# Later slots for one head's attention products and delta chain, and its DMA transposes issued from ScalarE's queue

## The reference

```
h = rms_norm(x); one projection h @ w_in gives, for each of 8 heads of width 128,
   q, k, v, gate path of a causal attention (with 256 tokens there is one block: plain causal softmax with ALiBi)
   q, k, v, gate path of a gated delta rule (short causal conv + SiLU on q, k, v), and two merge gates of 2048
A: softmax(q k^T - slope * distance) v * silu(z)                       -> ya, 1024 wide
B: delta rule in chunks, per-head rms_norm * silu(z)                   -> yb, 1024 wide
merged = sigmoid(g_a) * (ya @ w_branch_a) + sigmoid(g_b) * (yb @ w_branch_b)
out = rms_norm(x + merged @ w_out)
```

## Time and profile before

| | |
|---|---|
| median of 3 runs | 788.77 us (787.17 to 788.86) |
| the profiled execution's own time | 788.17 us, of which its span is 786.4 us |
| TensorE's granted clock | 0.998 of full speed over the span |
| busy: PE, DVE, ACT, POOL | 764.7, 553.3, 467.6, 102.1 us |
| moved by DMA | 152.89 MB, at a mean of 194 GB/s |

### The profile page before, as it was taken

One profiled execution on the slowest core, in us unless ns is written; L12 is line 12 of the kernel. 1 busy time (PEld: TensorE's weight loads), 2 busy tenths in 40 slices (PEclk: granted clock), 3 DMA queues, 4 the chain that ended last, 5 costly groups with the idle time before them and its releaser, 6 DMA issues.

```text
span 786.4 us, 10433 instructions
## 1 busy us (share of the span) xinstructions
PE 764.7 (97%) x3507; PEld 627.6 (80%) x3507; DVE 553.3 (70%) x1265; ACT 467.6 (59%) x697; POOL 102.1 (13%) x167
## 2 busy tenths in 40 slices
PE   8998999999999999999999999999999999999996
PEld 6887887888788878878887788788778888888884
DVE  5779748965895698479658956884797566765563
ACT  5686557656764766477567556764765764435440
POOL 5112010110101020101101010111020100001120
PEclk9999999999999999999999999999999999999999
DMA  9968757876687778668766877687676576688652
GB/s 250 247 169 199 201 161 188 220 193 173 184 221 198 177 194 209 174 177 219 193 172 179 214 207 172 180 206 201 172 193 199 176 197 189 181 264 272 192 160 108
DMA packets 219333, 152.89 MB, mean 194 GB/s; under 512 B 49168, under 2 KB 184336, under 8 KB 219152
## 3 DMA queue, kind: packets, MB, share of 16 engines
q1 hardware_dynamic: 219136, 151.96, 71.6%
q10 hardware_dynamic: 144, 0.26, 0.1%
HBM read 140.64 MB, written 2.11 MB: 182 GB/s over the span
## 4 chain that ended last, share of the span: by engine, by line
PE 67%; DMA 9%; ACT 8%; DVE 7%; SPq 5%; issue 4%; DVEq 0%; POOLq 0%; POOL 0%; ACTq 0%
PE pj L602 20%; PE pj L600 20%; PE pj L601 20%; DMA turned<-halves 9%; SPq L334 3%; DVE w_lo L1146 3%; ACT w_hi L865 2%; ACT moT L916 1%; ACT convs L935 1%; SPq L298 1%; ACT L947 1%; DVE kk L1299 1%; ACT yT L916 1%; PE pj L851 1%; PE pj L849 1%
## 5 line engine op out<-in xcount | busy, mean ns | idle before, releaser
L1146 DVE TENSOR_TENSOR w_lo<-w_raw,w_hi 128x1024 fp32r<-128x1024 f32 x251 | 307.5, 1230 | 157.3 <-ACT w_hi L865 155.9
L600 PE MATMUL pj<-w_hi,xt_hi 128*128 128x512 f32 x860 | 345.9, 402 | 0.4 <-DVE w_lo L1146 0.4
L602 PE MATMUL pj<-w_hi,xt_lo 128*128 128x512 f32 x860 | 336.6, 391 | 0.0
L601 PE MATMUL pj<-w_lo,xt_hi 128*128 128x512 f32 x860 | 335.9, 391 | 0.0
L865 ACT ACTIVATE w_hi<-w_raw 128x1024 fp32r<-128x1024 f32 x251 | 263.5, 1054 | 118.4 <-PE pj L602 106.6
L602 PEld LDWEIGHTS pj<-w_hi,xt_lo 128*128 128x128 f32 x860 | 161.4, 188 | 34.3
L600 PEld LDWEIGHTS pj<-w_hi,xt_hi 128*128 128x128 f32 x860 | 161.8, 188 | 32.2 <-issue 0.6
L601 PEld LDWEIGHTS pj<-w_lo,xt_hi 128*128 128x128 f32 x860 | 161.9, 188 | 31.1
L1333 DVE SCALAR_TENSOR_TENSOR xs<-lrep,xs 128x31 f32<-128x31 f32 (+30 forms) x496 | 80.0, 231 | 0.0
L535 POOL TENSOR_TENSOR xo<-v,own 128x128 f32<-128x128 f32 x16 | 14.7, 919 | 125.3 <-DVE v L1342 87.3
L1273 DVE SCALAR_TENSOR_TENSOR conv<-kk,hs,conv 128x255 f32<-128x255 f32 (+2 forms) x72 | 29.7, 475 | 0.0
(11 more groups left out here) (292 smaller groups left out, 734.6 us busy)
## 6 DMA issues: line engine op xcount, KB each, us to landing
w_raw<-in_w_in_dram SPq DMA_DIRECT2D x384, 256.0 KB, 3.4
w_raw<-in_w_out_dram SPq DMA_DIRECT2D x64, 256.0 KB, 3.7
w_raw<-in_w_branch_a_dram SPq DMA_DIRECT2D x32, 256.0 KB, 3.6
w_raw<-in_w_branch_b_dram SPq DMA_DIRECT2D x32, 256.0 KB, 3.7
gate<-in_x_dram SPq DMA_DIRECT2D x8, 256.0 KB, 5.3
gate<-in_x_dram SPq DMA_DIRECT2D x4, 512.0 KB, 7.1
gate<-in_final_norm_gain_dram SPq DMA_DIRECT2D x1, 1024.0 KB, 9.4
out_dram<-gate SPq DMA_DIRECT2D x4, 256.0 KB, 3.5
```

Of the source, the lines that this page charges most:

```text
L600: pe.matmul(bank[:, t, :], hi[:, k, tok], w_hi[:, slot, cs], start=(k == 0), stop=False)
L601: pe.matmul(bank[:, t, :], hi[:, k, tok], w_lo[:, slot, cs], start=False, stop=False)
L602: mm = pe.matmul(bank[:, t, :], lo[:, k, tok], w_hi[:, slot, cs], start=False, stop=(k == kt_all - 1))
L1146: dve.tensor_tensor(w_lo[:, slot, :], w_raw[:, slot, :], w_hi[:, slot, :].bitcast(F32), ALU.subtract).then_inc(lo_ready, 1)
```

## The change

The table of slots moves. The products with k come one slot later (28 to 29), and with them the whole chain of the delta rule (`SUB`, `S_V`, `S_Y` to `S_O` each by one). The attention's join, q k^T, exp, transposes, products and output move two slots later (`M_JOIN` 37 to 39, `M_QK` 38 to 40, and so on to `M_YT` 51 to 53); `M_NAT` and `M_HALVES` stay. `S_SILU` stays at 26, and the join of the transposed delta output goes from slot 24 of the next head to slot 27 (`S_YT` 72 to 75), which is behind the SiLU instead of ahead of it.

All five transposes leave SP. ACT issues each one itself, behind the copy that writes the halves, and waits for that copy first; for `back` there is a new slot, `S_GO_BACK = 37`. In branch A the unit (0, 3), which needs the last head's attention output, changes places with (1, 0).

```diff
-S_NAT, ..., S_SILU, S_KK, S_BACK = 15, 17, 18, 21, 22, 24, 26, 28, 42
+S_NAT, ..., S_SILU, S_KK, S_GO_BACK, S_BACK = 15, 17, 18, 21, 22, 24, 26, 29, 37, 43
-J_YA, J_DN, J_YB, J_MO, J_BACK = 5, 14, 16, 22, 23
-SUB = {33: (0, 2), 34: (2, 4), ...
+SUB = {34: (0, 2), 35: (2, 4), ...
-S_Y, S_XY, S_XT = [48, 54], [50, 56], 52
-S_Y0, S_R1, S_Y1, S_O, S_YB, S_YT = 59, 61, 63, 65, 68, 72
+S_Y, S_XY, S_XT = [49, 55], [51, 57], 53
+S_Y0, S_R1, S_Y1, S_O, S_YB, S_YT = 60, 62, 64, 66, 69, 75
-M_NAT, M_HALVES, M_JOIN, M_QK, M_EXP, M_PT, M_PV, M_YA, M_YT = 31, 33, 37, 38, 40, 42, 44, 46, 51
+M_NAT, M_HALVES, M_JOIN, M_QK, M_EXP, M_PT, M_PV, M_YA, M_YT = 31, 33, 39, 40, 42, 44, 46, 48, 53
+A_ORDER = [(0, 0), (0, 1), (0, 2), (1, 0), (0, 3), (1, 1), (1, 2), (1, 3)] + [(c, j) for c in (2, 3) for j in range(4)]
 # SP
-                    turned_behind(h, j)
 # ACT
+            def turn_y(landed):
+                act.dma_start_transpose(turned[:, 0:4, :], halves[:, 0, :]).then_inc(landed, 16)
 ...  (S_HALVES)
+                    act.wait_ge(dn_halves_ready, T * (h + 1))
+                    act.dma_start_transpose(dn_halvesT, ...).then_inc(dn_landed, 16)
+                if s == S_GO_BACK:
+                    act.wait_ge(back_halves_ready, h + 1)
+                    act.dma_start_transpose(back_halvesT, ...).then_inc(back_landed, 16)
 ...  (S_YB, M_YA)
+                    act.wait_ge(yb_halves, h + 1)
+                    turn_y(yb_landed)
 ...  (M_HALVES)
+                    act.wait_ge(mo_halves_ready, T * (h + 1))
+                    act.dma_start_transpose(turned[:, :, :], ...).then_inc(mo_landed, 16)
```

More of the change, by code:

```diff
@@ L35 @@
 FIRST_O = FIRST_B + NC * BU
+A_ORDER = [(0, 0), (0, 1), (0, 2), (1, 0), (0, 3), (1, 1), (1, 2), (1, 3)] + [(c, j) for c in (2, 3) for j in range(4)]
+A_LAST = [max(n for n, (at, _) in enumerate(A_ORDER) if at == c) for c in range(NC)]
 LEVELS = 2
@@ L287, in _ @@
         def _(sp):
[L288 to L307, removed]
             sp.dma_start(gains[:, :], norm_gain.rearrange("(k c) -> k c", c=P)).then_inc(rows_landed, 16)
@@ L363, in chunk, with load @@
             def chunk(wmat, c, units, first_unit):
-                col = c * CH
                 for j in range(units):
[L367 to L381, removed]
+                    load(wmat, c * CH, j, c * units + (first_unit + j))
+            def load(wmat, col, j, number):
+                sp.wait_ge(lo_ready, number - RING + 1)
+                for i in reversed(range(UK)):
+                    k = UK * j + i
+                    sp.dma_start(w_raw[:, number % RING, i * CH:(i + 1) * CH],
+                                 wmat[k * P:(k + 1) * P, col:col + CH]).then_inc(w_landed[number % RING], 16)
+            for n, (c, j) in enumerate(A_ORDER):
+                load(w_a, c * CH, j, FIRST_A + n)
             for c in range(0, NC):
@@ L772, in _, with free, between @@
                 iteration(h, False)
[L774 to L793, removed]
+            for n, (c, j) in enumerate(A_ORDER):
+                def free(t, c=c):
+                    if c == 0:
+                        pe.wait_ge(gate_ready, T * (H - 1) + t + 1)
+                    elif c == 1:
+                        pe.wait_ge(mo_nat_ready, T * H)
+                    else:
+                        pe.wait_ge(a_gated, T * (c - 2) + t + 1)
+                def between(t, n=n):
+                    dn_step(T * n + t + SLOTS, H - 1)
+                if n == A_ORDER.index((0, BU - 1)):
+                    pe.wait_ge(ya_lo_ready, H)
+                unit(n % RING, FIRST_A + n, ya_hi, ya_lo, UK * j, pj[c % 2], H, free, between)
             def turn_merged(c):
@@ L1015, in mo_step @@
                                        ACT.Copy).then_inc(mo_halves_ready, 1)
+                    act.wait_ge(mo_halves_ready, T * (h + 1))
+                    act.dma_start_transpose(turned[:, :, :], halves[:, :, :].rearrange("p e n -> p (e n)")).then_inc(mo_landed, 16)
                     if not first:
@@ L1454, in gate_b @@
                     dve.tensor_tensor(g, g, gate[:, c, t, :], ALU.add).then_inc(merged, 1)
[L1456 to L1464, removed]
+            for n in range(NC * BU):
+                dn_step(2 * n + SLOTS, H - 1)
+                mo_step(2 * n + SLOTS, H - 1)
+                tail_split(FIRST_A + n + LEAD)
+                dn_step(2 * n + 1 + SLOTS, H - 1)
+                mo_step(2 * n + 1 + SLOTS, H - 1)
+                if n - 2 in A_LAST:
+                    gate_a(A_LAST.index(n - 2))
             def merged_lo(c):
```

14 lines of the change are left out of this document (9 added, 5 removed).

## The result

The changed kernel takes 800.75 us (799.8 to 801.22, 4 runs) against 788.34 us (787.17 to 788.86, 4 runs) of the kernel before: 1.58% slower, ratio 1.0158, 95% interval 1.014 to 1.0176. The profiled execution has a span of 798.1 us against 786.4. I had forecast 790.5 us in a range of 781 to 797: the sign was the likeliest one, the size was outside the range.

A forecast was written before the change was run, and what follows sets the result against it. PE, busy 764.7 of 786.4 us, was taken as the bound. Seven heads gain 2.15 us of new waits (15.0), 12.9 us go: 788.17 + 2.1 = 790.3 profiled, forecast 790.5 us, range 781 to 797.

The forecast's parts named there:

- The wait before q k^T: PE's wait for the join of the transposed halves; claimed to go in all 8 heads, giving back 8.6 us.
- The price of an issue: Time a transpose's issue holds ACT, taken from SP's rows as 1.44 and 1.20 us; said to decide the result.
- The walk through slots 16 to 27: Head 5 followed from ACT's output copy to the SiLU; PE waits 1.25 us before the products with k, against 0.68.
- The third wait: PE before the second small product, for ACT's late copy of `ysb` behind `ya`'s issue: about 0.5 us a head.
- The second new wait: exp: PE before the probabilities' transposes: chain of 23.1 us behind the products with k, wanted at 22.62; wait about 0.4 us.
- the wait at the products with k: PE waiting there for the SiLU, delayed by two issues and the way over `ro`: 1.25 us in seven heads.
- rival 3: Issues on two queues slow each other: 794 to 800 us, 797 at 0.3 us more per issue; chance 0.28.
- a rival's figure: Rival that an issue hardly holds ACT, all three new waits go: 775 to 778 us; chance 0.12.

The follow-up runs named there:

- e5: The changed kernel with the join of the back halves on ACT (slot 41) instead of POOL's copy: 792.08 us, ratio 1.0061 to the kernel before.
- e2: The changed kernel's new slots and branch A order, but all transposes issued by SP as in the kernel before: 773.80 us, ratio 0.9828 to that kernel.
- e1: The changed kernel with POOL's copy of the back halves held back until the same head's scores are done: 796.81 us, ratio 1.0117 to the kernel before.
- e8: The changed kernel, yb's transposes issued behind the SiLU, ya's behind the copy of ysb, back halves joined on ACT: 775.89 us, ratio 0.9842 to the kernel before.
- e3: The kernel before with its old slots and only the transposes' issues moved to ACT (back at slot 36): 794.81 us, ratio 1.0095.

## Why the prediction was wrong

**What held.** The wait before q k^T went whole. The price of an issue was read off SP's rows and was right (1.21 and 1.56 against 1.20 and 1.44 us). The walk through slots 16 to 27 came out to a tenth: from the end of the halves (406.70 in the prediction, 414.22 in head 5 of after) I had `ro` 4.23 us, the SiLU 14.87 and the products with k 15.96 behind; the rows have 4.24, 14.95 and 16.04. The waits there were forecast at 7 x 1.25 = 8.8 us and cost 3.9 + 5.4 = 9.3. The third wait was forecast at 7 x 0.5 = 3.5 us and cost 4.1 in 8 heads: head 0 has it too, since its `ya` and `ysb` are its own.

**The step that failed** is a term of "The second new wait: exp": "From the kk tiles to the scores took 15.1 us without the 0.47 wait; it gets six more `SUB` operations of 0.15, 16.0." The other terms were right. From the products with k: kk tiles 4.48 forecast, 4.45 measured; from the scores to the transposes 2.6 and 2.53; PE wants them at 22.62 and 454.21 - 1.40 - 430.26 = 22.55. The term itself was 16.97 instead of 16.0 (451.68 - 434.71; 16.9 in each of the other heads), and since the margin was already used up, all 0.97 us became wait of PE: 1.40 us in this head instead of about 0.4. Over all heads the wait cost 9.8 us against 2.8, which is 7.0 of the 9.5 us that the forecast was short (790.3 against 799.8 of the profiled execution); 0.6 are the third wait, about 0.6 the wait at the products with k, and 1.3 the longer distances between L574 and L575.

**Why it was 16.97.** I moved DVE's operations and took their durations along as if nothing beside them moved: what POOL's copy adds was put at nothing, without a reason. But the diff moves `back`'s issue, and with it POOL's copy, from beside the scores into the `SUB` chain. SP's timeline of before has that issue in head 5:

```profile
433.45 1.24 SPq L307 DMA_TRANSPOSE dn_nat<-conv  x1
```

Before, it was issued 12.7 us behind the products with k and POOL's copy came 5.4 us later; after, 10.5 and 3.3 (440.71 and 444.03). One `SUB` per head then stands 1.32 us. e5, which takes the copy off POOL, brings the group back to 80.6 us, the term to 15.9 and the wait to 0.2 us a head: the cause is shown. The trace of before had the sign of it: the operation on `mx` beside which the copy lay then takes between 168 and 905 ns:

```profile
L1392 DVE TENSOR_SCALAR mx<-mx x8: 168/286/905, 76.5 to 586.3; 128x2 f32<-128x2 f32 x8
```

The Trainium skill has the rule on its page "SBUF — State Buffer", section "SBUF: two separate sides": VectorE and GpSimd share a pair of ports under an exclusive lock, taken by a GpSimd operation or by a VectorE operation that has two SBUF inputs (this only against a GpSimd operation that reads SBUF, as the copy does) or runs in a mode with two ports, and the one that comes second stands until the first is done. The runs agree: not many `SUB`s a little slower, but one in each head, of up to 1324 ns, beside a copy of 1.35 us, and none in e5; and the other way round the `xo` of e2 that wait for a split. That the operation on `mx`, with one input, was blocked as well in e1 fits only if it runs in a mode with two ports, which no row shows.

**The rivals and the range.** I gave rival 3, issues that slow each other on two queues, 0.28, and it ended at the right side for the wrong reason: the issues took 1.21 and 1.56 us, 0.01 and 0.12 more than on SP, where the rival asked for 0.3. By its own sign, issues of over 1.5 us, one of the two kinds met it, but 0.12 us is 0.8 us over seven heads. The range stopped at 797 because I summed only known prices at their upper ends. With a margin of 0.4 us gone at one place and 0.5 at the next, any further delay of DVE counts eight times, 8 us for each microsecond, and that slope should have set the upper end, not the price of an issue alone. Nor did the prediction ask what the later slots would give without the other half; e2 shows that it is a gain of 13.6 us, which the issues on ACT turned into a loss.

The rule that I cited from the Trainium skill, page "DMA: Bandwidth & Descriptors", section "Issuing engines are not separate DMA queues", that the time to start a transfer is usually small relative to it, led to 775 us as a rival's figure. The runs disagree in this case for the price (1.21 to 1.56 us beside landings of 3.4 to 5.6 us). That e8 comes to 775.9 does not bear the rule out: its issues are as long, but two of five in a head run beside other work of ACT, and no wait of PE stands behind the other three.

## What to carry to other kernels

An issue from a compute engine's queue costs what stands behind it on that engine: put it behind the operation that somebody waits for, or leave it to a queue on which nothing waits; here the same five issues cost 27 us or 2. And do not put it right behind the copy whose result it sends, where it must wait for the copy and leaves the engine idle (1.28 us here); issued some operations later, it ran beside the engine's own work. When a change moves a transfer, follow what its landing releases on every engine, and look what it will lie beside: a copy on POOL costs nothing on POOL's account and a microsecond on VectorE's, and only where VectorE has no slack left. And test the halves of a combined change apart, since one may be a gain of 1.7% hidden under the other.

## What the runs showed that I had not expected

How long a landing takes does not follow from the issuing engine alone. Median us from issue to landing, first after, then e2:

```profile
turned<-halves ACTq DMA_TRANSPOSE x24, 4.0
...
conv<-convs ACTq DMA_TRANSPOSE x8, 5.6
dn_nat<-conv ACTq DMA_TRANSPOSE x8, 3.4
```

```profile
turned<-halves SPq DMA_TRANSPOSE x24, 4.0
conv<-convs SPq DMA_TRANSPOSE x8, 3.7
dn_nat<-conv SPq DMA_TRANSPOSE x8, 4.6
```

The transposes into `conv` land 1.9 us later from ACT's queue in after, but in e3, also from ACT, they take 3.9; those into `dn_nat` take 3.4 in after and 5.7 in e3. Why is open.
